# Low parts of the weight sums on VectorE, and one root moved into the last normalisation, in the feed-forward stage of a decoder step

## What is computed

```
hp = rms_norm(y_p, g_ffn_pre[l])
y_p = y_p + rms_norm(swiglu(hp, w_gate[l], w_up[l], w_down[l]), g_ffn_post[l])

def rms_norm(x, g):
    xf = x.astype(jnp.float32)
    xf = xf * lax.rsqrt(jnp.mean(jnp.square(xf), axis=-1, keepdims=True) + RMS_EPS)
    return (xf * g.astype(jnp.float32)).astype(x.dtype)
def swiglu(hn, w_gate, w_up, w_down):
    return (jax.nn.silu(hn @ w_gate) * (hn @ w_up)) @ w_down
```

## Time and profile before

| | |
|---|---|
| median of 3 runs | 1031.74 us (1026.45 to 1033.98) |
| profiled execution | 1032.12 us, span of the records 1030.3 us |
| busy, share of the span | PE 89%, DVE 71%, ACT 45%, POOL 39% |
| eight results of the first pair | on PE until about 585 us |
| units 0 to 31 | 585 to 1016 us |
| closing work | 1016 to 1030 us |

### The profile page before, as it was taken

One profiled execution on the slowest core, in us unless ns is written; L12 is line 12 of the kernel. 1 busy time (PEld: TensorE's weight loads), 2 busy tenths in 40 slices (PEclk: granted clock), 3 DMA queues, 4 the chain that ended last, 5 costly groups with the idle time before them and its releaser, 6 DMA issues.

```text
span 1030.3 us, 17813 instructions
## 1 busy us (share of the span) xinstructions
PE 922.1 (89%) x7150; PEld 841.4 (82%) x7150; DVE 731.0 (71%) x1244; ACT 466.6 (45%) x849; POOL 398.1 (39%) x261
## 2 busy tenths in 40 slices
PE   5999999898999999999999859879988869988797
PEld 4999988665998899765899858869987769978786
DVE  4799883655446961225348998986899995599976
ACT  5543315755544631453355445444544433444452
POOL 3000001111000342001100647779977778877770
PEclk9999999899999999999998969889999989999899
DMA  8232116431523592763120041222312222222232
GB/s 238 88 96 84 42 54 215 144 103 41 169 83 118 169 316 94 273 258 101 63 83 1 1 169 42 83 82 82 103 62 83 82 82 82 83 82 72 62 119 87
DMA packets 81556, 110.56 MB, mean 107 GB/s; under 512 B 9505, under 2 KB 64674, under 8 KB 81090
## 3 DMA queue, kind: packets, MB, share of 16 engines
q1 hardware_dynamic: 81248, 109.37, 31.9%
q10 hardware_dynamic: 226, 0.05, 0.0%
HBM read 100.48 MB, written 8.93 MB: 106 GB/s over the span
## 4 chain that ended last, share of the span: by engine, by line
PE 63%; DVE 29%; ACT 3%; issue 3%; DMA 1%; SPq 1%; DVEq 0%; POOL 0%; ACTq 0%
PE pall L2188 19%; PE pall L2762 16%; PE pall L2200 5%; PE pall L2542 4%; DVE w_sum L1349 4%; PE pall L2225 3%; DVE g_part_f L1349 3%; DVE g_part_f L1343 3%; DVE w_sum L1346 2%; DVE tt L1343 2%; DVE w_raw L1349 2%; DVE g_part L1349 2%; DVE gate_odd L1343 2%; PE pall L2593 1%; PE pall L2258 1%
## 5 line engine op out<-in xcount | busy, mean ns | idle before, releaser
L760 POOL TENSOR_TENSOR ring_lo<-w_raw,ring_hi 128x512 fp32r<-128x512 f32 (+1 forms) x128 | 189.6, 1493 | 131.0 <-ACT ring_hi L1218 129.7
L760 POOL TENSOR_TENSOR ring_lo<-w_sum,ring_hi 128x512 fp32r<-128x512 f32 (+1 forms) x96 | 147.0, 1538 | 33.7 <-ACT ring_hi L1218 33.6
L2762 PE MATMUL pall<-g_part,ring_hi 128*128 128x272 f32 x616 | 126.1, 304 | 16.8 <-DVE g_part L1349 13.1
L2762 PE MATMUL pall<-x_hi,ring_hi 128*128 128x272 f32 x320 | 99.3, 310 | 31.3 <-DVE sq L1346 22.4
L2762 PEld LDWEIGHTS pall<-g_part,ring_hi 128*128 128x128 f32 x616 | 103.4, 202 | 19.5 <-DVE g_part L1349 13.8
L2762 PE MATMUL pall<-x_sum,ring_hi 128*128 128x272 f32 x480 | 95.4, 294 | 18.1 <-ACT gate_odd L1246 13.1
L2762 PE MATMUL pall<-x_lo,ring_hi 128*128 128x272 f32 x320 | 97.3, 304 | 0.0
L2762 PE MATMUL pall<-x_hi,ring_lo 128*128 128x272 f32 x320 | 97.2, 304 | 0.0
L2762 PEld LDWEIGHTS pall<-x_sum,ring_hi 128*128 128x128 f32 x480 | 76.7, 192 | 21.2 <-ACT gate_odd L1246 14.9
L2762 PEld LDWEIGHTS pall<-x_hi,ring_hi 128*128 128x128 f32 x320 | 65.3, 204 | 35.0 <-DVE sq L1346 24.3
L708 POOL TENSOR_TENSOR w_lo<-w_raw,w_hi 128x2048 fp32r<-128x2048 f32 x7 | 32.0, 4570 | 157.3 <-PE pall L2648 79.2
(11 more groups left out here) (441 smaller groups left out, 2386.2 us busy)
## 6 DMA issues: line engine op xcount, KB each, us to landing
w_raw<-in_w_gate SPq DMA_DIRECT2D x10, 1024.0 KB, 5.3
w_raw<-in_w_up SPq DMA_DIRECT2D x10, 1024.0 KB, 5.4
w_raw<-in_w_in SPq DMA_DIRECT2D x8, 1024.0 KB, 5.8
w_raw<-in_w_down SPq DMA_DIRECT2D x8, 1024.0 KB, 5.1
dm_kv<-in_cache_mem_v SPq DMA_DIRECT2D x5, 1024.0 KB, 13.8
w_raw<-in_w_out SPq DMA_DIRECT2D x4, 1024.0 KB, 8.5
d_k<-in_cache_k SPq DMA_DIRECT2D x16, 256.0 KB, 2.9
d_v<-in_cache_v SPq DMA_DIRECT2D x16, 256.0 KB, 4.0
```

The costliest lines, as they stand in the source:

```text
L760: e.tensor_tensor(w_part(ring_lo[:, q % RING, :], n), sev_source(n, i), w_part(ring_hi[:, q % RING, :], n).bitcast(F32), ALU.subtract)\
L2762: ins = mm(out, w, x, start=i in SEV_FIRST and j == 0 and s_, stop=j == np_ - 1 and t_, skip_group_check=i not in SEV_FIRST)
```

## The change

Five edits, all in the feed-forward stage:

1. The low parts of products 1, 2 and 5 move from POOL (`sev_lo`) to DVE (`sum_low`). POOL keeps those of 0, 3, 4 and 6. In DVE's list the low parts 1 and 2 of unit n + 1 stand in front of `sev_evac(n)`, the low part 5 inside it, ahead of the addition after product 5. Waits on the low parts become `low_ready`. `sums_in_banks` returns False, so all sums stay in `w_sum` as before.
2. The two multiplications of the silu tiles by `rstd` are dropped. The whole feed-forward result is then too large by a factor 1/`rstd` per token, which the last normalisation cancels, provided RMS_EPS is divided by the square of `rstd`: in unit 28 (the first of the last four) DVE sets `sqacc_y` to EPS/128 over `rstd` squared (a product, a reciprocal and a scaling, 128x544 each, each awaited), the squares are added to that (one more addition), and the root loses its bias.
3. In front of the list, DVE makes all four low parts of the input sums. Four of the eight `pair_half` are dropped: `first_pair` reads the up half from PSUM.
4. Units use banks 0, 1, 5 and 2, 3, 4 in turn. Unit 0 starts after four `pair_half`, unit 1 after two operations of `first_pair`.
5. The first pair's high and low parts (`g_hi`, `g_low` of pair 0) move behind unit 0: on DVE from unit 0's part of the list to the start of unit 1's.

```diff
+    def low_ready(n, i):
+
+        if i in (1, 2, 5):
+            return S("sum_lo"), 3 * n + (1, 2, 5).index(i) + 1
+        return S("sev_lo"), 4 * n + (0, 3, 4, 6).index(i) + 1
...
-        for q in range(7 * len(sev)):
-            if q in (3, 5):
...
-            sev_lo(q)
+        for n in range(len(sev)):
+            for i in (0, 3, 4, 6):
+                sev_lo(7 * n + i)
...
+        def sum_low(n, i):
+
+            if n == len(sev):
+                return
+            q = 7 * n + i
+            e.wait_ge(S("sev_hi"), q + 1)
+            sub(w_part(ring_lo[:, q % RING, :], n), sev_source(n, i), w_part(ring_hi[:, q % RING, :], n).bitcast(F32)).then_inc(S("sum_lo"), 1)
...
+            e.wait_ge(S("x_sum_lo"), 4)
+            e.wait_ge(acc_full, J_FFN + 8)
             e.wait_ge(S("silu"), 2)
-            mul(b11, sq[:, 0, H0], tt[:, 0, H0])
-            mul(b22, sq[:, 1, H1], tt[:, 1, H1]).then_inc(S("g_made"), 1)
-            mul(b21, sq[:, 1, H0], tt[:, 1, H0])
-            done(mul(sq[:, 0, H1], sq[:, 0, H1], tt[:, 0, H1]))
+            mul(b11, up[0], tt[:, 0, H0]).then_inc(acc_out, 1)
+            mul(b21, up[1], tt[:, 1, H0]).then_inc(acc_out, 1)
+            mul(sq[:, 0, H1], up[2], tt[:, 0, H1]).then_inc(acc_out, 1)
+            mul(b22, up[3], tt[:, 1, H1]).then_inc(acc_out, 1)
...
         e.wait_ge(S("rstd_half"), 1)
-        for i in range(4):
-            pair_half(i)
+        pair_half(0)
+        pair_half(1)
         weight_sums(0, (1, 2))
         y_even = yT[:].rearrange("p (j k) (a t) -> p j k a t", k=2, a=2)
         done(sub(x_sum_f[:, 0, 1], y_even[:, :, 0, 1, :], y_even[:, :, 0, 0, :]))
         recip_half("n4", 1)
         input_sum(0)
         input_sum(1)
+        input_low(0)
         e.wait_ge(S("rstd_half"), 2)
         pair_half(4)
         pair_half(5)
         input_sum(2)
-        pair_half(6)
+        input_low(1)
         input_sum(3)
-        pair_half(7)
+        sum_low(0, 1)
+        sum_low(0, 2)
         input_low(2)
+        sum_low(0, 5)
         weight_sums(1, (1, 2))
         input_low(3)
         first_pair()
...
+            if n == 1:
+                for i in range(3):
+                    g_low(0, i)
...
             if adds:
                 sev_add(n, 1)
+            sum_low(n + 1, 1)
+            if adds:
                 sev_add(n, 2)
-            if before == "gate":
-                for m in range(2):
-                    e.wait_ge(S("silu"), 2 * p + m + 1)
-                    mul(gate_tile(p, m), gate_tile(p, m), rstd[:])
-            if n == 0:
-                for i in range(3):
-                    g_low(0, i)
+            sum_low(n + 1, 2)
             last = what == "down" and at_[0] == LAST_DOWN
-            if last and at_[1]:
+            if last and at_[1] == 0:
+                done(mul(sqacc_y[:], rstd[:], rstd[:]))
+                done(e.reciprocal(sqacc_y[:], sqacc_y[:]))
+                done(e.tensor_scalar(sqacc_y[:], sqacc_y[:], EPS / P, None, ALU.mult))
+            elif last:
...
             sev_evac(n)
+            if n == 0:
+                sum_low(1, 5)
```

More of the change, by code:

```diff
@@ L321, in sev_banks, with sums_in_banks, w_sums @@
     def sev_banks(n):
-        return [bank(3 * (n % 2) + i)[:, 0:HALF] for i in range(3)]
+        return [bank(i)[:, 0:HALF] for i in ((2, 3, 4) if n % 2 else (0, 1, 5))]
+    def sums_in_banks(n):
+        return False
+    def w_sums(n):
+        first = (bank(6), bank(7)) if sums_in_banks(n) else (w_sum[:, 0, :], w_sum[:, 1, :])
+        return [w_part(t, n) for t in (*first, w_sum[:, 2, :])]
+    def low_ready(n, i):
+        if i in (1, 2, 5):
+            return S("sum_lo"), 3 * n + (1, 2, 5).index(i) + 1
+        return S("sev_lo"), 4 * n + (0, 3, 4, 6).index(i) + 1
     SEV_BANK = (0, 2, 0, 1, 0, 2, 0)
@@ L1214, in sev_hi @@
             if i in (1, 2, 4, 5):
-                e.wait_ge(S("w_sum"), 4 * n + (None, 1, 3, None, 2, 4)[i])
+                made = (None, 3, 4, None, 2, 4) if sums_in_banks(n) else (None, 1, 3, None, 2, 4)
+                e.wait_ge(S("w_sum"), 4 * n + made[i])
             else:
@@ L1325, in _ @@
         e.wait_ge(*counted("n5", "sum", 1))
-        e.activation(small[:, Y_RSTD:Y_RSTD + 4], bank(4)[:, 0:4], ACT.Sqrt, bias=small[:, EPS_COL:EPS_COL + 1]).then_inc(S("norm_root"), 1)
-        e.activation(small[0:NS_TOK, Y_RSTD + 4:Y_RSTD + 5], bank(4)[0:NS_TOK, 4:5], ACT.Sqrt,
-                     bias=small[0:NS_TOK, EPS_COL:EPS_COL + 1]).then_inc(S("norm_root"), 1)
+        e.activation(small[:, Y_RSTD:Y_RSTD + 4], bank(4)[:, 0:4], ACT.Sqrt).then_inc(S("norm_root"), 1)
+        e.activation(small[0:NS_TOK, Y_RSTD + 4:Y_RSTD + 5], bank(4)[0:NS_TOK, 4:5], ACT.Sqrt).then_inc(S("norm_root"), 1)
     @block.vector
@@ L1950, in weight_sums @@
             a11, a12, a21, a22 = (quarter(n, k, m) for k, m in ((0, 0), (1, 0), (0, 1), (1, 1)))
-            s1, s2, s4 = (w_part(w_sum[:, i, :], n) for i in range(3))
+            s1, s2, s4 = w_sums(n)
             if 1 in which:
@@ L2052, in sev_evac @@
                 mul(u1[:, H1], u1[:, H1], rstd[:, H1])
+            if n:
+                sum_low(n + 1, 5)
             ended(5)
@@ L2780, in _ @@
         zg_transposes(KT - 1)
-        e.wait_ge(*counted("n5", "add", KT - 1))
+        e.wait_ge(*counted("n5", "add", KT))
         for t in range(5):
```

55 lines of the change are left out of this document (28 added, 27 removed).

## The result

| | before | after |
|---|---|---|
| median | 1031.7 us (1026.45 to 1033.98, 4 runs) | 1001.86 us (997.79 to 1005.22, 4 runs) |
| ratio | | 0.9716, 95% interval 0.9657 to 0.9776 |
| span of the profiled execution | 1030.3 us | 1002.9 us |

A forecast was written before the change was run, and what follows sets the result against it. The prediction took DVE, with its waits for POOL at the shared port, to bound the gate and up units. Gains of 16 + 7 + 1.5 - 5 = 19.5 us against the profiled 1032.12 gave 1012 us, range 997 to 1028.

The forecast's parts named there:

- What bounds it: Gate and up units: DVE sets the pace, busy 27.81 of 28.2 us, partly waiting for POOL's low parts.
- DVE's own work: Gate and up pair: 17.0 us counted before; 11.2 us left as waits for POOL's 14 low parts, 0.80 each.
- A: From DVE's addition after product 4 of a gate unit to the up unit's: 13.6 us to 11.4, nine gain 20.
- B: From the up unit's addition after product 4 to the next gate unit's: grows by 0.6 us, seven cost 4.
- The clock: Gate and up units: A 10.9 us by DVE or 11.9 with a fall of PE's clock; the middle, 11.4, taken.
- DVE waiting for ACT: `sum_low` makes DVE wait in order for ACT's high part; claimed to cost nothing.
- In front of the list: Before and in units 0 and 1: input sums freed of POOL's long operations, less 2 for `g_low(0)`; gain 7 us.
- Down units: Down units: PE waits only 0.31 us a unit in the middle group; gain 1.5 us.
- The last group: From unit 28 on: added DVE work, product 6 of unit 28 waits some 2.5 us; loss 5, from 2 to 8.
- More hides: Gate and up units: the shared port alone sets the pace, 24.5 us a pair, kernel 997 us; chance 0.19.
- The clock takes it: Gate and up units: PE's clock falls after each B; kernel 1027 us, with half of each 1023; chance 0.18.
- slower: Low parts on DVE wait for late ACT high parts, 2.4 us a unit; kernel 1050 us; chance 0.11.

The follow-up runs named there:

- the repeat: The changed kernel run again, unedited, on another chip: 1005.26 us, ratio 0.9747 to the kernel before.
- half width: Changed kernel with POOL's low parts cut to half their columns from unit 2 on, the rest left out: 972.69 us, ratio 0.9447 to the kernel before.
- four low parts: Changed kernel with product 0's low part moved to DVE too from unit 2 on, three left on POOL: 998.21 us, ratio 0.9687 to the kernel before.
- the full move: Changed kernel with all seven low parts a unit on DVE from unit 2 on, POOL idle there: 987.6 us, ratio 0.9584 to the kernel before.

## Why the prediction came out as it did

**What bounds it: right.** DVE did set the pairs, through POOL's turns at the shared port. With POOL's operations cut to 16 columns the pair fell to PE's 21.1 us, all else equal.

**DVE's own work: the term that was mis-sized.** The prediction multiplied counts by durations and got 17.0 us before and 19.7 after; measured with POOL at rest they are 15.7 and 18.0. It left 11.2 us of waits for 14 POOL operations and called that 0.80 each; it is 12.5, or 0.89. The two errors cancel in the pair before, by which they were fitted. After it they don't: 19.7 + 8 x 0.80 = 26.1, 18.0 + 8 x 0.89 = 25.1, measured 24.8. So 1.0 of the 1.3 us missed per pair is this term. The other 0.3 is that a POOL operation cost 0.85 here; why less than before was not separated.

**A and B: the step that failed.** It subtracted a modelled stretch from a measured one. By its own model the stretches before are 7.07 + 7 x 0.80 = 12.7 and 9.93 + 5.6 = 15.5; measured were 13.6 and 14.6. The sum fits, the split doesn't, and the forecast of B growing by 0.6 came from setting 15.2 against 14.6. In the pair shown B shrank by 1.0.

What the split had wrong is how POOL's operations lie; it took them as even. The forecast gave A 7.7 + 4 x 0.80 and B 12.0 + 4 x 0.80; it is 7.0 + 5 x 0.85 and 11.0 + 3 x 0.85. So A was right by luck: 0.7 too much of own work against 1.0 too little of POOL. In B both errors have one sign, 1.0 and 0.6, and make the 1.6 us by which it was missed.

Summed over the list, stretch by stretch, nine A gave 23.3 us where 20 were forecast. The six B that lie within these stages (the prediction's seventh is in units 0 and 1) gave 3.4 where 4 were to be lost; not every B shrank by 1.0, the least by 0.1. Together 26.6 against the 25.9 of the table; by groups 5.9, 12.6 and 8.1 against 5.9, 12.7 and 7.3.

**The clock: the middle was taken, and it didn't dip.** The reason given for a dip was the wait of 2.83 us in front of A; after, no wait between two units of a pair is longer than 1.5 us, and the clock is 1.00 in every gate and up stretch. But the wait alone never decided it. The kernel before has six of 2.81 to 2.83 us. In the 2 us behind them the granted clock was 0.50 twice, 0.62, 0.78, and 1.00 twice. Two of them, columns as in the earlier trace rows:

```profile
679.90:681.90 2.00, 2.00 (x18) 2.00 (x18) 2.00 (x3) 0.12 (x1) 2.00 (x3) 1.00 0.00 0
808.20:810.20 2.00, 2.00 (x10) 2.00 (x10) 2.00 (x3) 0.19 (x1) 2.00 (x3) 0.50 0.00 0
```

**DVE waiting for ACT: right for the pairs.** No wait of `sum_low` there. The prediction put this at nothing by the time at which ACT is done; the 9.7 us in 19 waits lie in down units and right behind them, where DVE is early anyway.

**In front of the list: right size, wrong cause.** The forecast had 7 and units 0 and 1 gave 7.2. But it gave the gain to the input sum and took 2 back for `g_low(0)`. The input low parts are worth nothing, and moving `g_low(0)` out of unit 0 is worth 3.6. Product 6 was forecast near 603 and came at 606.56, 2.7 of which is the late front.

**Down units: near in size, another cause.** They gave 2.5 for 1.5. The forecast took it from waits of 0.31 us inside the units; 2.2 of the 2.5 are the wait for `g_part` at the head of the first two groups, 4.57 us before and 3.47 and 3.48 after.

**The last group: the stall right, the total near.** 2.80 for a stall of 2.5, and +5.4 for +5 (+8.1 in the repeat, at the lower clock). Removing the long reciprocal removes the stall. PE's waits grew by 6.0 in this stage in all, at a slightly higher clock (0.94 against 0.91): 2.8 at the stall, and 3.2 where PE waits for `zg_out`, which the forecast had as 1.7 + 0.9; then, not in the forecast, 1.3 at an earlier addition of unit 28 and 0.2 elsewhere, less 1.6 at `g_part`.

**The rivals.** "More hides" gave 24.5 a pair and 997 us; 24.8 and 1001.9 lie nearer to it than to the forecast's 26.1 and 1012. Its mechanism, only work at the port counting, isn't shown by that: the sum of the own work and of POOL's cost gives the same pair, and the runs that were to part the two theories (half width, four low parts) measured between them. "The clock takes it" fell by the windows at 1.00, "slower" by the waits.

**The signs.** Of those named for being right, the stall in unit 28 and shorter 512-column operations came. The pair was below the 26 to 27 us, and POOL's busy time fell by 151 us, more than the 140 named. None of those for being wrong came.

## What to carry to other kernels

Size an engine's list by the distance between starts in a stretch where it runs back to back, not by durations, and measure a shared resource's cost against that; a fit to one total lets two wrong terms cancel. Let a model reproduce the parts of the kernel before, not only the sum, before you subtract it from them. Work on POOL is not free cover for DVE: where both read two tiles in SBUF, what DVE loses to the port (0.9 us) can exceed what it saves (0.60), and the full move was worth more than the half.

## What the runs showed of the hardware

- DVE operations of 512 columns start 0.60 us apart under records of 0.68 us (0.72 between some of the weight sums), those of 272 columns 0.35 under 0.43.
- A POOL subtraction of 128x512 costs DVE 0.85 to 0.94 us, though it runs 1.29 alone, both with POOL at work for 22 of 27 us and for 13 of 25 (0.76 in the run where three a unit were left and DVE waits for PE in each pair). At half width it costs about 0.4: (21.5 - 0.3 of waiting - 15.7) / 14 = 0.39, (22.0 - 1.0 - 18.0) / 8 = 0.38.
- A reciprocal of 128x544 takes 3.55 us, one of 128x4 0.18; an operation on 4 columns still took up to 0.71.
- After a PE wait of 2.81 to 2.83 us the granted clock in the next 2 us was anything from 0.50 to 1.00. Where the pairs wait in pieces of at most 1.5 us it stayed at 1.00 in all three stretches of gate and up units.
